# Expert units of a mixture-of-experts stage as a short nested loop, with gate and up stored by blocks of 128 columns

## The reference

```python
def swiglu(x, wg, wu, wd):
    return (jax.nn.silu(x @ wg) * (x @ wu)) @ wd

def moe_swiglu(x, w_router, wg, wu, wd):     # 8 experts, wg and wu 1024x2816, wd 2816x1024
    logits = (xt @ w_router).astype(jnp.float32)
    top_v, top_i = lax.top_k(logits, TOP_K)   # TOP_K = 2
    top_w = jax.nn.softmax(top_v, axis=-1)
    gate = jnp.sum(jax.nn.one_hot(top_i, N_EXPERTS) * top_w[..., None], axis=1)
    for e in range(N_EXPERTS):
        out = out + gate[:, e:e + 1] * swiglu(xt, wg[e], wu[e], wd[e])
```

## Time and profile before

| | |
|---|---|
| median of three runs | 1736.87 us |
| the profiled execution's own time | 1737.35 us |
| its span, first to last instruction | 1735.5 us |
| expert stage, first unit to last | 942.5 to 1710.7 us |
| DMA, all | 408.95 MB, mean 236 GB/s |
| TensorE busy | 1598.7 us, 92% |

### The profile page before, as it was taken

How to read it: one execution, slowest core, us unless ns; L and a number is a source line. 1 busy time by engine, 2 the same in 40 slices (tenths; PEclk the granted TensorE clock), 3 DMA queues, 4 the chain that set the end, 5 groups by cost and what they waited for, 6 DMA issues and landing times.

```text
span 1735.5 us, 59237 instructions
## 1 busy us (share of the span) xinstructions
PE 1598.7 (92%) x27333; PEld 1411.3 (81%) x27333; DVE 531.3 (31%) x1261; ACT 300.5 (17%) x708; POOL 16.4 (1%) x32
## 2 busy tenths in 40 slices
PE   5999898999989999999678999999999999999996
PEld 3888587997457879888567989898989899998985
DVE  1464326766373436655335100000000101000001
ACT  2112322001023314343214001010101000010001
POOL 1000000000000000000000000000000000000000
PEclk8999999999989999999978999999999999999997
DMA  9822858545592440000423999999999999999980
GB/s 355 265 98 87 293 216 268 189 148 193 170 279 72 141 141 5 6 5 7 170 70 108 369 350 367 368 346 366 366 364 364 358 366 373 347 379 376 346 307 26
DMA packets 175313, 408.95 MB, mean 236 GB/s; under 512 B 13107, under 2 KB 86245, under 8 KB 175077
## 3 DMA queue, kind: packets, MB, share of 16 engines
q1 hardware_dynamic: 170480, 398.91, 63.9%
q0 software_dynamic: 1184, 3.41, 0.6%
q10 hardware_dynamic: 3412, 2.93, 0.5%
HBM read 403.31 MB, written 1.92 MB: 233 GB/s over the span
## 4 chain that ended last, share of the span: by engine, by line
PE 47%; PEld 40%; issue 5%; DVE 4%; DMA 2%; ACT 2%; SPq 0%; DVEq 0%; POOL 0%; ACTq 0%; PEldq 0%
PEld bank L1417 25%; PEld bank L1438 12%; PE bank L955 8%; PE bank L988 4%; PE bank L629 3%; PE bank L632 3%; PE bank L732 2%; PE bank L735 2%; PE bank L1167 2%; PE bank L1127 2%; PE bank L655 2%; PE bank L757 2%; PE bank L1163 2%; PE bank L1152 2%; PE bank L1103 2%
## 5 line engine op out<-in xcount | busy, mean ns | idle before, releaser
L1417 PEld LDWEIGHTS bank<-w,ring 128*64 128x64 f32 x11264 | 437.1, 138 | 38.4 <-issue 37.4
L1417 PE MATMUL bank<-w,ring 128*64 128x88 f32 x11264 | 448.7, 240 | 19.6 <-issue 18.6
L1438 PE MATMUL bank<-w,ring 128*64 128x88 f32 x5632 | 224.6, 240 | 14.9 <-issue 14.6
L1438 PEld LDWEIGHTS bank<-w,ring 128*64 128x64 f32 x5632 | 217.1, 137 | 21.0 <-issue 20.2
L2720 DVE TENSOR_TENSOR w<-w,bank 128x352 f32<-128x352 f32 (+1 forms) x48 | 22.1, 488 | 614.1 <-PE bank L1417 614.1
L1914 ACT ACTIVATE w<-bank 128x352 f32<-128x352 f32 (+1 forms) x48 | 19.3, 438 | 461.8 <-PE bank L1417 461.7
L629 PE MATMUL bank<-w,ring 128*128 128x256 f32 x256 | 59.1, 394 | 4.3 <-DVE w L2396 3.7
L629 PEld LDWEIGHTS bank<-w,ring 128*128 128x128 f32 x256 | 50.5, 198 | 13.0 <-DVE w L2396 4.0
L632 PE MATMUL bank<-ring,w 128*128 128x256 f32 x256 | 57.8, 389 | 0.9 <-DVE w L1978 0.9
L655 PE MATMUL bank<-ring,ct 128*32 128x256 f32 x768 | 48.9, 405 | 9.0 <-DMA ring<-in_ada_w 6.8
L632 PEld LDWEIGHTS bank<-ring,w 128*128 128x128 f32 x256 | 50.0, 196 | 8.4 <-DVE w L1978 1.3
(11 more groups left out here) (434 smaller groups left out, 1968.4 us busy)
## 6 DMA issues: line engine op xcount, KB each, us to landing
ring<-in_moe_w_gate SPq DMA_DIRECT2D x88, 1024.0 KB, 6.9
ring<-in_moe_w_up SPq DMA_DIRECT2D x88, 1024.0 KB, 7.3
ring<-in_moe_w_down SPq DMA_DIRECT2D x88, 1024.0 KB, 7.6
ring<-in_ada_w SPq DMA_DIRECT2D x48, 1024.0 KB, 5.6
ring<-in_ev_w_in SPq DMA_DIRECT2D x11, 1024.0 KB, 13.5
ring<-in_ffn_w_gate SPq DMA_DIRECT2D x11, 1024.0 KB, 7.9
ring<-in_ffn_w_up SPq DMA_DIRECT2D x11, 1024.0 KB, 5.5
ring<-in_ffn_w_down SPq DMA_DIRECT2D x11, 1024.0 KB, 6.5
```

The source lines that it names most:

```text
L1417: ins = [mm(b[hp, (a % 4) * CAP:(a % 4 + 1) * CAP], w[:, k, a * P + hp.start:a * P + hp.stop], XG[:, kk, :], start=kk == 0 and a % 4 == 0, ...
L1438: ins = [mm(bank[4 + c // 4][hp, (c % 4) * CAP:(c % 4 + 1) * CAP], w[:, k, c * P + hp.start:c * P + hp.stop], HIDU[:, s % 2, 2 * part + k, :],
```

## The change

A block is now 128 hidden columns, and there are 22 blocks in a unit. Gate and up of a block lie together in one new input tensor, `moe_gu`, in which each partition's 8 KB are contiguous; it is laid out before the launch. The down weights of a block are 128 rows, half a slot. TensorE's order in a unit becomes: gate_up(0) with turn_y between its halves, both scatters, gate_up(1), down(0), the turned selection, then a loop of 5 passes with 4 times [gate_up(t), down(t-1)], gather, down(21). The seven units are one outer loop. All thresholds of waits become functions of the loops' registers. The gather works by half columns, and `CAP` is 86.

```diff
-CAP = 88
+CAP = 86
-STEPS = (1024, 1024, 512, TW)
-UT = 33
+HB = 22
+ROWS, LOOPS = 4, 5
+UT = 3 * HB
+UNIT_TILES = [("gu", 0), ("gu", 1), ("d", 0)]
+for _t in range(2, HB):
+    UNIT_TILES += [("gu", _t), ("d", _t - 1)]
+UNIT_TILES += [("d", HB - 1)]
+def moe_slot(kind, t):
+    if kind == "gu":
+        return EXPERTS[t if t < 2 else 3 + 2 * ((t - 2) % ROWS)]
+    return EXPERTS[2 if t in (0, HB - 1) else 4 + 2 * ((t - 1) % ROWS)]
...
+                for n, (kind, b) in enumerate(UNIT_TILES):       # SP
+                    slot = ring[:, moe_slot(kind, b), :]
+                    if kind == "gu":
+                        dst, src = slot, t["moe_gu"][bass.ds(e, 1), b].rearrange("a p n -> (a p) n")
+                    else:
+                        dst = slot[:, D:2 * D] if b == HB - 1 else slot[:, 0:D]
+                        src = t["moe_w_down"][0][bass.ds(e, 1), b * P:(b + 1) * P, :].rearrange("a k n -> (a k) n")
+                    free = n - RING + 1 if u is None and n < RING else moe_free(kind, b)
+                    at = N_MOE + free if u is None else u * UT + (N_MOE + free)
+                    sp.wait_ge(sem("tile_used"), at)
+                    sp.wait_ge(sem("tile_used0"), at)
...
-                        ins = mm(bank[6 + c // 4][:, (c % 4) * CAP:(c % 4 + 1) * CAP], HTM[:, st, c * P:(c + 1) * P],
-                                 SEL[:, st, :], start=st == 0, stop=st == 1)
+                        ins = [mm(bank[6 + c // 4][hp, (c % 4) * CAP:(c % 4 + 1) * CAP],
+                                  HTM[:, st, c * P + hp.start:c * P + hp.stop], SEL[:, st, :],
+                                  start=st == 0 and c % 4 == 0, stop=st == 1, skip_group_check=True) for hp in HALVES]
...
+                def gate_up(t, due, between=lambda: None):
+                    slot = moe_slot("gu", t)
+                    pe.wait_ge(sem(f"slot{slot}"), due)
+                    w = ring[:, slot, :].rearrange("p (w k n) -> p w k n", w=2, k=KC)
+                    across(bank[t % 2], w[:, 0])
+                    between()
+                    across(bank[2 + t % 2], w[:, 1])
...
+                with pe.Fori(0, LOOPS) as i:
+                    for t in range(2, 2 + ROWS):
+                        slot, slot_d = moe_slot("gu", t), moe_slot("d", t - 1)
+                        gate_up(t, u * (16 * LOOPS) + i * 16 + (due0[slot] + 16))
+                        down(t - 1, f"slot{slot_d}", u * (16 * LOOPS) + i * 16 + (due0[slot_d] + 16),
+                             u * HB + i * ROWS + (FT + t))
...
-            for u in range(NE - 1):
+            with pe.Fori(0, NE - 1) as u:
                 unit(u)
```

## The result

The changed kernel takes 1666.86 us (median of 4 runs, 1664.41 to 1670.7) against 1734.64 for the kernel before (4 runs): a ratio of 0.961, 95% interval 0.958 to 0.964. It is faster by 68 us where 32 were forecast, and the time lies under the forecast's range of 1694 to 1720 and under the wider one of 1682 to 1745. The profiled execution has a span of 1662.6 us.

What follows compares the result with a forecast made beforehand. TensorE, short of instructions, was taken as the bound, DMAs just behind. TensorE's side of 90.5 us a unit alone gave 1694; supply at 375 GB/s ended units at 1679 against 1710.7, 32 less: 1705 us, range 1682 to 1745, likeliest 1694 to 1720.

Steps and rivals of the forecast that it cites:

- Bound before: Expert stage: TensorE with its instruction supply is the bound, 5 us of stalls in a unit of 95.6 us; DMAs just behind.
- part 1's gain: TensorE's short loop stays in the engine's memory, nothing is fetched in seven of eight units, stalls go: -5.0 us a unit.
- Part 5, the supply: Expert stage's loads: 267.9 MB from 958 us at 375 GB/s (bounds 355 and 407) take 714 us; units end at 1679.
- third rival: Supply rises above 383 GB/s, so TensorE is the bound: 1690 to 1694 us, or 1682 if jumps are free; chance 0.13.
- The late start of loads: Start of expert stage: the next load waits until the third gate-and-up block is done, about 15.5 us in; loads start at 958.
- Part 1's price of a jump: TensorE's loops: 0.3 us a jump back, 5 inner and 1 outer, +1.8 us a unit; lower bound 0.
- Pace: TensorE's halves with 86 tokens in the expert stage: 37.6 ns each.
- TensorE's side: TensorE's time for a unit after the change: 90.6 + 1.8 + 1.5 - 0.3 - 1.7 - 1.4 = 90.5 us.
- Parts 2 to 4: Per unit: head +1.5 us (scatters -0.3), 86 tokens -1.7 us, gather by half columns -1.4 us.
- Second rival: TensorE's loop isn't held and each jump back fetches anew, 4.8 us a jump: about 1920 us; chance 0.17, half for partly held.

Runs made afterwards that it cites:

- `a_stream`: The changed kernel with both of TensorE's loops written out (seven units and the 20 inner blocks unrolled): 1779.9 us, ratio 1.026.
- `a_body9`: The changed kernel with the first of five inner passes written out and four looped, a unit's body some 2,150 instructions: 1770.5 us, ratio 1.022.
- `a_half`: The changed kernel with half of the gate and up products left out, so that the DMAs alone bound the stage; only its time counts: 1628.44 us.
- `a_cap88`: The changed kernel with 88 tokens a unit again in place of 86: 1680.11 us, ratio 0.969.
- `a_inner_out`: The changed kernel with TensorE's inner loop of 20 blocks written out and the outer loop over the units kept: 1835.86 us, ratio 1.056.
- `a_late`: The changed kernel with a unit's head reordered: gate and up of block 0, turning, gate and up of block 1, then both scatters: 1659.1 us, ratio 0.956.

## Why the prediction was wrong, step by step

- **Bound before, part 1's gain: right.** TensorE starved for instructions, the loops are held, q8 is silent, the stalls go. `a_stream` confirms the cause and `a_body9` its limit. The size has a slip: 768 us over 8 units is 96.0 us, not 95.6, so with TensorE alone as the bound the sum gives 1691, not 1694. The forecast of 1705 came from the supply and does not move.
- **Part 5, the supply: the step that failed.** It took 375 GB/s between the rates of the earlier trace rows, as if a share of 0.99 made them a ceiling, though TensorE had no wait for data. `a_half` shows 418 GB/s, and the changed kernel draws 394 with no wait for data. So the third rival, with a chance of 0.13, was the case: TensorE alone. The 11 us that the forecast added for the supply (1694 to 1705; 14 with a unit of 96.0) do not exist. The late start of loads does: 41 GB/s from 945 to 958 us. It cost nothing, since the supply then ran at 414 to 1027 us and TensorE was busy all that time. The 358 GB/s of the Trainium skill, which the prediction cites, do not agree with 418 over 400 us either.
- **Part 1's price of a jump: mis-sized, and the larger term.** 0.3 us x 6 a unit were charged, 14 us in all; the timeline shows no idle at one. The row it was sized by, held a load from memory besides. Nought was its lower bound.
- **Pace.** 37.6 ns a half were taken, 37.3 measured; 2,176 halves make it 0.7 us a unit. With the jumps this is 2.5 of the 2.75 us by which a unit is shorter than the 90.5 of TensorE's side.
- **Parts 2 to 4: right.** Head 1.5 forecast, 1.17 + 0.2 in the timeline. 86 tokens -1.7 a unit, and `a_cap88` gives 1.5 from unit to unit, 13.3 / 8 = 1.7 over all. The gather -1.4, measured 1.5.
- **Outside the units** another 3.2 us went: the last scatters run at 0.43 us a MATMUL, before at 0.86 (granted clock 0.71 against 0.58 from the end of the units to the end). This was not foreseen, and why the clock fell sooner before is not shown.
- **Second rival: wrong for this body, right as a mechanism.** It took 4.8 us a missed jump. The runs show 7 us of idle (`a_inner_out`) and 10.5 (`a_body9`), and a lower clock behind it. The rule of the Trainium skill ("Runtime: NRT & Kernel Launch", section "Instruction fetch mechanics") of a window of two pages does not agree: 1,380 instructions, more than five packets, are held. The Trainium skill, "Advanced Engine Details and Errata", section "ISA Cache", gives TensorE 128 KB (by 64 bytes an instruction, as its 16 KB for 256 make it, 2,048), and that fits between 1,540 held and 2,150 not held; its "Only 2 cache lines" does not.

The third rival's own time was missed too. It said 1690 to 1694, or 1682 with free jumps, where 1694 less 14 is 1680. The stage is how the time came out: in the profiled executions it lasts 768 us before (942.5 to 1710.7) and 701 after (939.7 to 1641.0), 67 less. It starts 3 us earlier, which may be chance (`a_late`, the same up to there, starts at 942.1), and 3 us go behind it. 1737.4 less 73 is 1664.4, as the profiled execution has it; the median is 1666.9.

Of the 41 us between the forecast's 1705 and that execution, the jumps are 14, the supply 14 (the slip of 3 among them), the pace 5, the end 3, and some 4 are left over. Jumps and supply are the two terms that put the time outside the range.

## What to carry to other kernels

A DMA share near 1 is no ceiling while something else sets the pace: look for a wait of the engine on a landing, compare the time a packet takes with the shortest in the trace, or leave out work and measure the ceiling. Idle by "issue" after every 128 matmuls is missing instructions; a loop whose whole body is held removes it, and a body that is too long gives nearly all of it back (1770 us at 2,150 instructions, and 1836 with the inner loop written out, above the 1780 without any loop). Idle rows alone undercount what the stalls cost: 11.3 us of idle a unit went with a unit that was 14.3 us longer.

## What the runs showed that was not expected

- Weights and instructions compete: with the same instructions stream, full loads cost 1780 us, half loads 1673, a sixteenth 1662.
- A body of 2,150 instructions runs at 1770 us, one of 1,380 at 1667, one written out altogether at 1780.
- A missed jump of TensorE costs 7 to 10.5 us of standing still and then a granted clock of 0.50 for some microseconds.
- Jumps of TensorE into a held body leave no idle between matmuls.
- The DMAs sustain 418 GB/s with gate and up in runs of 8 KB and 410 with runs of 4 KB, rows 11 KB apart, over 400 us.
